# Storing the turned keys and queries one pair of weight blocks earlier in SyncE's order

## The reference, cut to what matters

```
h = rmsnorm(x, g_mix)
z = h @ w_in                                  # (576, 1024) x (1024, 8192)
rq, rk, rv, rg, dq, dk, dv, gr, gd = split(z)
rq, rk = rotary(rq), rotary(rk) * 128**-0.5   # retention queries and keys
dq, dk = rmsnorm(dq, g_q), rmsnorm(dk, g_k)   # attention queries and keys, per head
o_d = softmax(dq1 dk1') v - lam softmax(dq2 dk2') v     # 4 heads, chunk-causal
o_r = retention(rq, rk, rv)                              # 4 heads
x = x + (sig(gr) * W_ret(silu(rg) * norm(o_r)) + sig(gd) * W_diff(norm(o_d))) @ w_out
x = x + moe(rmsnorm(x))                       # 4 groups of 4 experts, top 2 of one group
```

## Time and profile before

| | |
|---|---|
| time, median of 3 runs | 1004.96 us (1004.31 to 1008.19) |
| the profiled execution | 1006.94 us, of which the span of the trace is 1005.0 us |
| TensorE busy with matmuls | 985.7 us, 98% |
| TensorE weight loads, VectorE, ScalarE, GpSimd | 81%, 68%, 53%, 15% |
| granted TensorE clock, mean | 0.994 of full speed |

### The profile page before, as it was taken

One profiled execution on the slowest core, in us unless ns is written; L12 is line 12 of the kernel. 1 busy time (PEld: TensorE's weight loads), 2 busy tenths in 40 slices (PEclk: granted clock), 3 DMA queues, 4 the chain that ended last, 5 costly groups with the idle time before them and its releaser, 6 DMA issues.

```text
span 1005.0 us, 12193 instructions
## 1 busy us (share of the span) xinstructions
PE 985.7 (98%) x4638; PEld 814.2 (81%) x4638; DVE 683.2 (68%) x1007; ACT 528.3 (53%) x724; POOL 150.9 (15%) x184
## 2 busy tenths in 40 slices
PE   9999999999999999999999999999999999999995
PEld 6888888877888888877878888789788888888884
DVE  6586875347767763543458447686989898898883
ACT  6744322345555653332452314544688786887782
POOL 1010001121120311121130000012012121121111
PEclk9999999999999999999999999999999999999998
DMA  9476567873461655974284345137899999999994
GB/s 353 138 220 146 134 141 233 253 232 116 169 222 56 247 204 187 350 274 149 94 322 156 105 186 212 53 128 305 347 400 404 380 404 388 396 405 380 404 398 72
DMA packets 125988, 245.28 MB, mean 244 GB/s; under 512 B 69072, under 2 KB 69376, under 8 KB 113600
## 3 DMA queue, kind: packets, MB, share of 16 engines
q1 hardware_dynamic: 105520, 172.51, 47.2%
q0 software_dynamic: 20112, 71.37, 21.6%
q10 hardware_dynamic: 288, 0.52, 0.1%
HBM read 203.07 MB, written 52.08 MB: 254 GB/s over the span
## 4 chain that ended last, share of the span: by engine, by line
PE 55%; issue 27%; DVE 7%; ACT 4%; POOL 3%; SPq 2%; DMA 1%; POOLq 0%; ACTq 0%; DVEq 0%
PE ps L486 13%; PE ps L488 13%; PE ps L487 13%; PE ps L1902 3%; PE ps L1903 3%; SPq L602 2%; PE ps L1875 2%; DVE w_lo L422 2%; ACT w_hi L417 1%; POOL x_exp L871 1%; DVE neg_max L1503 1%; POOL out_y L882 1%; ACT prob L1151 1%; PE ps L2050 1%; PE ps L2066 1%
## 5 line engine op out<-in xcount | busy, mean ns | idle before, releaser
L486 PE MATMUL ps<-w_hi,s_hi 128*128 128x512 f32 x640 | 252.0, 394 | 0.0
L488 PE MATMUL ps<-w_lo,s_hi 128*128 128x512 f32 x640 | 249.5, 390 | 0.0
L487 PE MATMUL ps<-w_hi,s_lo 128*128 128x512 f32 x640 | 249.4, 390 | 0.0
L488 PEld LDWEIGHTS ps<-w_lo,s_hi 128*128 128x128 f32 x640 | 120.1, 188 | 25.3
L486 PEld LDWEIGHTS ps<-w_hi,s_hi 128*128 128x128 f32 x640 | 120.3, 188 | 24.2 <-issue 0.3
L487 PEld LDWEIGHTS ps<-w_hi,s_lo 128*128 128x128 f32 x640 | 120.3, 188 | 23.7
L422 DVE TENSOR_TENSOR w_lo<-raw,w_hi 128x2048 fp32r<-128x2048 f32 x40 | 91.6, 2289 | 45.3 <-ACT w_hi L417 45.2
L1029 ACT ACTIVATE stage<-ps,x_rstd 128x512 f32<-128x512 f32 x64 | 44.0, 687 | 131.2 <-PE ps L488 130.7
L417 ACT CAST w_hi<-raw 128x2048 fp32r<-128x2048 f32 x40 | 76.0, 1904 | 15.5 <-DMA raw<-in_w_in 10.0
L458 DVE TENSOR_TENSOR lo_x<-raw_x,hi_x 128x2048 fp32r<-128x2048 f32 x32 | 72.4, 2284 | 6.3 <-ACT hi_x L435 6.3
L488 PE MATMUL ps<-lo_x,x_hi 128*128 128x512 f32 x192 | 75.6, 394 | 0.0
(11 more groups left out here) (318 smaller groups left out, 1890.6 us busy)
## 6 DMA issues: line engine op xcount, KB each, us to landing
raw<-in_w_in SPq DMA_DIRECT2D x30, 1024.0 KB, 8.1
raw_x<-in_w_gate SPq DMA_DIRECT2D x30, 1024.0 KB, 23.8
raw_x<-in_w_down SPq DMA_DIRECT2D x18, 1024.0 KB, 23.1
raw_x<-in_w_up SPq DMA_DIRECT2D x16, 1024.0 KB, 20.6
raw<-in_w_up SPq DMA_DIRECT2D x16, 1024.0 KB, 21.3
raw<-in_w_down SPq DMA_DIRECT2D x14, 1024.0 KB, 22.7
x_slots<-in_c_empty SPq DMA_DIRECT2D x4, 2112.0 KB, 19.5
x_exp<-x_slots POOLq DMA_DIRECT2D x16, 528.0 KB, 13.0
```

Source lines behind the costliest of these rows:

```text
L486: nc.tensor.matmul(out, s_h, w_h, start=first, stop=False)
L487: nc.tensor.matmul(out, s_l, w_h, start=False, stop=False)
L488: return nc.tensor.matmul(out, s_h, w_l, start=False, stop=last)
```

## The change

Each `store_turned(c)` moves one pair of loads up in SyncE's order: from behind load 2c + 7 to behind load 2c + 5. So for chunk 0 it stands between loads 5 and 6 instead of between 7 and 8, and so on to chunk 5, between loads 15 and 16 instead of between 17 and 18. What is stored, its waits and the other engines' programs stay as they are.

```diff
         for n in range(4, N0):
             dense_load(n)
-            if n % BPC == 1 and n // BPC - 3 in DVE_CHUNKS:
-                store_turned(n // BPC - 3)
+            if n % BPC == 1 and n // BPC - 2 in DVE_CHUNKS:
+                store_turned(n // BPC - 2)
             g = n - FILL_AT
```

## The result

The changed kernel takes **1039.77 us** (median of 3 runs, 1038.62 to 1040.18) against 1004.96: a ratio of 1.033, 95% interval 1.0308 to 1.0351. By the medians it is 34.8 us slower, by the ratio 33. The forecast was 1029, with a range of 1012 to 1044. The profiled execution took 1040.18, its span 1038.3 us, so against the span before (1005.0) the trace has 33.3 us to explain.

What follows compares the result with a forecast made beforehand. TensorE, busy 985.7 of 1005.0 us, bounds the kernel; late loads can only slow it. Tile 4 of chunk 7 23.6 us late, less 1 given back, plus 1.4 clock, makes 24: 1004.96 + 24 = 1029 us, range 1012 to 1044.

Steps and rivals of the forecast that it cites:

- Loads behind stores: On SyncE, 20 store issues stand between the free slot and the pair of loads; 1029 us, chance 0.80.
- a round longer than a chunk: Store run 10.9, second landing 9.0, cast 1.9, low part to turn's end 5.05: 26.85 us against 25.4.
- waits of TensorE at tile 4: TensorE idle before tile 4 of each chunk, growing by round, longest in chunks 6 and 7; 23.6 us late at the last.
- the collisions: Store runs of chunks 4 and 5 beside GpSimd's transfers: 7.0 and 7.75 us added, half of each as lower bound.
- The first round: Nearly free at tile 4 of chunk 2: bank free at 78.7 to 80.7 against 79.08, hardly any cast wait.
- GpSimd's wait for the last store: GpSimd's 19.1 us wait before loading the first values at the start of attention was to go.
- store runs of chunks 0 to 3: SyncE's 20 issues, with weights landed before the run starts, cost 10.9 us, against 15.6 to 15.9 before.
- from the pair's issue to the next run: Landing 9.0, cast 1.9, low part to turn's end 5.05; 2 us added in the first round for GpSimd's store.
- The landing of the pair: Second load, issued behind a store run, lands 8.0 to 10.0 us after the first's issue; 9.0 taken.
- The clock: TensorE's clock falls behind the waits; covered inside a round, 1.4 us lost at the last one.
- Rival three: Clock falls at every wait and stays in the loop: 1.4 us in each of six rounds, 1036 us; chance 0.07.
- Given back: First values in time for the first head of attention: 0 to 2 us gained, 1 taken.

Runs made afterwards that it cites:

- the turn made early: Changed kernel with VectorE's turn moved from behind the second low part to ahead of the first: 1004.02 us, 0.9981 of the kernel before.
- half of the issues: Against the changed kernel, ten of each chunk's 20 stores at the new place, ten at the old: 1008.11 us, 1.0024 of the kernel before.
- the run with the rotation behind the turn: Changed kernel with VectorE's rotation of tile 2 in chunks 4 and 5 moved behind the turn: 1034.33 us, 1.0288 of the kernel before.
- the run with the filler: Changed kernel with extra matmuls into an unused bank ahead of TensorE's four longest waits: 1034.52 us, 1.0283 of the kernel before.
- the early turn alone: Kernel before, SyncE's order kept, with VectorE's turn moved ahead of the first low part: 1006.83 us, 1.0009 of the kernel before.
- the wait behind the older stores: Against the changed kernel, older chunk's stores first at their old place, then the wait for the turn ahead of the pair: 1005.86 us, 1.0001 of the kernel before.

## Why the prediction was right, and where its sum was short

**The mechanism held.** Loads behind stores, a round longer than a chunk, waits of TensorE at tile 4 that are longest in chunks 6 and 7, the first values no longer late: each stands in the trace. Breaking the loop at two independent links removes the loss (the turn made early) or all but 2 us of it (half of the issues), while the wait, the store packets and the early turn by themselves do nothing.

Some of its signs came out otherwise. The waits at tile 4 don't grow steadily; the jump comes in the rounds with the collisions. The first round cost a wait of 2.65 us, where 0 to 1.6 was worked out, and ScalarE's cast waited 9.6 us for its load in it, where hardly any wait was expected. GpSimd's wait for the last store shrank by 4 us and did not go. And 6.4 of TensorE's 25.0 us of waits are at tile 1, a place that the forecast didn't have.

**The sum was 11 us short** by the medians, 9 by the traces (33.3 instead of 24; the profiled execution before was 2 us above its median, the one after 0.4). Tile 4 of chunk 7 is 32.65 us late where 23.6 was worked out. Term by term, from SyncE's queue:

| term of the sum | forecast | measured |
|---|---|---|
| turn of chunk 0 ends, stores begin | 59.74 | 59.92 |
| store runs of chunks 0 to 3 | 10.9 each | 10.69, 10.71, 11.00, 13.26 |
| store runs of chunks 4 and 5 | 17.9, 18.65 | 19.13, 19.05 |
| from the pair's issue to the next run | 17.95, then 15.95 four times | 18.71, 16.40, 17.13, 17.79, 16.08 |
| last pair's issue to tile 4 | 8.0 | 8.54 |

The runs are 3.7 us over in total, of which 2.4 in chunk 3's. That run overlaps GpSimd's four small loads at 151 us, but in the run with the rotation behind the turn they overlap it too and it takes 11.86; the cause stays open. From pair to run it is 4.4 over, mostly in the rounds of chunks 4 and 5: the step "cast 1.9, then from the start of the low part to the end of the turn 5.05" was taken from a chunk without rotation. In chunks 4 and 5 six VectorE operations stand between the two low parts, read here in chunk 4:

```profile
135.14 2.29 DVE L422 TENSOR_TENSOR w_lo<-raw,w_hi 128x2048 fp32r<-128x2048 f32 x1 [4.34 <-ACT w_hi L417]
137.35 0.42 DVE L1432 TENSOR_TENSOR rot_tmp<-stage,rot 128x256 f32<-128x256 f32 x1
...
139.16 0.42 DVE L1439 TENSOR_TENSOR stage<-rot_tmp 128x256 f32<-128x256 f32 x1
139.61 2.29 DVE L422 TENSOR_TENSOR w_lo<-raw,w_hi 128x2048 fp32r<-128x2048 f32 x1
141.82 2.84 DVE L1401 STREAM_TRANSPOSE turned<-stage 128x2560 f32<-128x2560 f32 x1
```

The second cast was done at 137.7; the low part waited until 139.61 for the rotation. Taking it out of the way removed this link in both rounds, and that kernel was 4 to 5 us faster (by the ratios and by the spans, 1033.2 against 1038.3), though not by this link alone, as its section says. The landing of the pair was sized rightly: worked out from the landings of the first load and of both, the second lands 8.2 to 9.0 us after the first's issue in rounds two to five, and some 11.3 in the first beside GpSimd's store, where the sum had 9.0 and 11.0.

**The range held partly by luck.** Its upper end came from a landing of 10.0 us and a loss by the clock in every round. Neither happened in that way; the store run of chunk 3 and the rotation, which the range didn't have, took up part of that room.

**The collisions** were sized rightly: 7.0 and 7.75 over a free run in the forecast, 8.2 and 8.1 measured against 10.9.

**The clock** cost 2.8 us in the last tile instead of 1.4, since it stayed low through nearly the whole tile, not nine matmuls. Rival three, the clock in every round, is half right: it fell in four places, but the run with the filler shows the loop covering the first of them.

**Given back** were 2.1 us, not 1, of which 1.8 in the first head, nearly the bound of 2 that was stated. One trace can't tell much here: in three other runs whose last stores end within 1.5 us of those of the kernel before (the early turn alone, the wait behind the older stores, half of the issues) TensorE's waits in that head come to 1.0, 0.8 and 2.2 us.

## What to carry to other kernels

Ahead of moving a transfer forward in an engine's hand-written order, list what stands behind it there, and ask whether the thing that it waits for depends on any of that: a wait, a run of issues and a load that feeds the same wait form a loop, and if its length is over the stage's period, it sets the pace of every round. The loss is then not a price per instruction but a threshold. Once the loop is open or shorter than the period, the loss is gone or nearly so (the producer moved ahead of the consumer of the late load; half of the issues); shortened but still longer, it only shrinks. And walk the loop's links in each stage that it passes: a link read from one stage was 2 us longer in another.

## What the runs showed of the hardware

Twenty issues on SyncE's queue take 10.7 us when no weights are ahead of them (0.53 us each), 15.6 to 15.9 when two loads of 1 MB were issued just before them, and 19 beside GpSimd's transfers: the issue itself is held, not only the data.

TensorE's granted clock fell after the waits of 3.2, 3.2, 6.4 and 7.6 us in the changed kernel: 0.66, 0.72, 0.69 and 0.53 on the mean of the 5 to 11 us around each, where matmuls started 0.43 us apart instead of 0.23. It didn't fall after those of 2.65, 1.1 and 0.6 us there (1.00 in these stretches). But with chunk 0 alone moved it fell after one of 3.1 us (0.66), and with chunks 0 to 3 moved after waits of 2.5 and 2.0 us (0.71, 0.69). In these traces the length of a wait alone doesn't tell whether the clock falls behind it.
